# A seam between two stages: the merge's loads are issued in the SSM stage, TensorE goes on without a meeting, and the projections are reordered

## The chip, the cores and the metric

The kernel runs on one NeuronCore of a Trainium2 chip, in one launch. The metric is the device time of an execution in microseconds, the median of several runs. The core has five engines that run their own instruction lists and meet only at semaphores: TensorE (PE, matmuls), VectorE (DVE), ScalarE (ACT), GpSimd (POOL) and SyncE (SP, which here issues every DMA). All data is fp32.

## What is computed

The reference is a first block, a mixer and a mixture of experts, followed by two layers of another block. The change lies in the mixer of the first block, at its merge. Cut to what matters:

```python
def mixer(hc, hl, p, rows, ctx_out):
    pl = jnp.einsum('bld,de->ble', hl, p['w_in'])
    rw_l, ss_l, gt_l = jnp.split(pl, IN_SPLITS, axis=-1)
    ya_c, ya_l = rwkv_branch(rw_c, rw_l, p, ctx_out)      # (1, 512, 1024)
    yb_c, yb_l = ssm_branch(ss_c, ss_l, p, rows, ctx_out)  # (1, 512, 2048)
    return merge(ya_l, yb_l, gt_l, p)

def merge(ya, yb, gates, p):
    ga, gb = jnp.split(jax.nn.sigmoid(gates), 2, axis=-1)
    ya = jnp.einsum('blc,cd->bld', ya, p['proj_a'])
    yb = jnp.einsum('blc,cd->bld', yb, p['proj_b'])
    return jnp.einsum('bld,de->ble', ga * ya + gb * yb, p['w_out'])
```

## The kernel before

The program is a row of stages: start, RWKV, SSM, merge, experts (MoE), and the two layers of the second block. At the end of a stage every engine calls `Port.meet`: it drains, raises its own end count and waits for the end counts of all engines. SyncE waits for all of them at the start of its part of the next stage.

**The stages around the change.** The RWKV stage writes its output to a DRAM buffer, `yad` (8 x 128 x 512). The SSM stage (`ssm_sync`, `ssm_tensor`, `ssm_vector` and so on) follows one list of steps, `ssm_order`, that all engines read. In it four groups of heads are convolved and scanned; a group's result is transposed and stored to `ybd` by `read` steps 4 to 7, a quarter of it each. SyncE does the store. Behind the last group's projection come 16 `mgate` blocks, the merge's gate projections: for each, TensorE does 8 matmuls, ScalarE copies the block out, SyncE stores it to `gmd`. The last of them share the list with the `read` steps of group 3, and the stage ends with a short chain: `yvar` on VectorE, `yrstd` on ScalarE, `dg` on VectorE, four matmuls with `ones` on TensorE (`yrstd`), and VectorE's copy of their result to `k.rb`.

**The merge stage** (`merge_sync`, `merge_tensor`, `merge_vector`, `merge_scalar`). For each of eight row blocks d of the output, TensorE computes `pa` d (8 matmuls of 128x128 by 128x512 over `yaT`) and `pb` d (16 matmuls over `ybT`), each into one of eight PSUM banks. VectorE multiplies both by their sigmoid gates, adds them into `mT[d]` and so frees the two banks. When all eight are there TensorE does the output projection `out` with four weight tiles `wo`. The profile has two records for each of these fp32 matmuls.

**What sets the order.** SyncE issues in program order and stops at each wait. Weights go through a `Ring`, slots of the area `wreg` used in turn: a load into a slot waits until the block that last used it is done. The SSM stage has two slots of 4096 words, the first two thirds of `wreg`; the last third holds its scan buffers. The merge has six slots of 2048 words over the same area. `gates(d)` loads the two gate blocks of d into one of two pairs of buffers and so waits for `mT[d-2]`. In the SSM stage two groups of buffers (`b.groups`) serve the four heads' groups in turn; groups 0 and 2 use the first, groups 1 and 3 the second.

Of the kernel before, what the change touches and what calls it, by code (L numbers as in the profile page):

```python
# [195 lines left out]
class Port:  # L196
# [5 lines left out]
    def wait_ge(self, line, *event):  # L202
# [4 lines left out]
        if self.seen.get(line.name, 0) < count:  # L207
            self.seen[line.name] = count
            self.e.wait_ge(line.sem, count)

    def meet(self, mine, stage):

        self.e.drain().then_inc(self.k.end[mine].up(stage), 1)
        for e in self.k.end:
            self.wait_ge(self.k.end[e], stage)

# [107 lines left out]
class Ring:  # L324


    def __init__(self, sp, areas):
        self.sp, self.areas, self.until, self.i = sp, areas, [None] * len(areas), 0

    def load(self, key, src, *until):  # L330
        i, k = self.i, self.sp.k
        self.i = (i + 1) % len(self.areas)
        if self.until[i]:
            self.sp.wait_ge(*self.until[i])
        self.until[i] = until
        dst = self.areas[i][:, 0:src.shape[1]]
        self.sp.e.dma_start(dst, src).then_inc(k.wline[i].up16(*(key if isinstance(key, tuple) else (key,))), 16)
        k.slot[key] = (dst, k.wline[i])


class Words:
# [45 lines left out]
def v3(ap, n):  # L387
    return ap.rearrange("p (a b) -> p a b", b=n)
# [80 lines left out]
def fetch(sp, dst, src, name):  # L469

    sp.e.dma_start(dst, src).then_inc(sp.k.line(name).up16(name), 16)
# [1004 lines left out]
def ssm_map(k):  # L1476
    b, m, extra, spare = Bag(), k.mem(k.mark1), k.mem(NC1 + NCOL + 8192), k.mem(k.mark0)
    b.hp = v3(m(4096), 512)
    k.rb_at = m.top
    b.dtb, b.na, b.dd = m(64), m(64), m(32)  # L1480
    b.dt, b.dA, b.sc, b.ecum, b.edec, b.etot = (m(384) for _ in range(6))
    b.ss = m(16)
    b.o2 = [m(768) for _ in range(2)]
    b.groups = []
    for _ in range(2):
        o = Bag()
        o.bcm, o.ccm, o.btok = m(768), m(512), m(768)
        o.xt, o.z, o.y = v3(m(3072), 512), v3(m(2048), 512), v3(m(2048), 512)
        b.groups.append(o)
    b.ysum = [m(512) for _ in range(2)]  # L1490
    b.ysq, b.yd = m(512), m(512)
    b.yo = [m(512) for _ in range(2)]
    b.stage = [m(512) for _ in range(2)]
    b.xd, b.xe = ([extra(512) for _ in range(2)] for _ in range(2))
    b.cbm = [extra(128) for _ in range(2)]
    b.h = [extra(512) for _ in range(2)]
    b.dg = extra(512)
    b.LB, b.Wt = ([spare(1024) for _ in range(2)] for _ in range(2))
    b.order = ssm_order()
    k.rb = k.mem(k.rb_at)(512)  # L1500
    return b
# [82 lines left out]
def ssm_sync(k, sp):  # L1584
    b, T, P = k.ss, k.T, k.proj
    for e in k.end:
        sp.wait_ge(k.end[e], "rwkv")
    fetch(sp, b.dtb, k.row("dtb"), "dtb")
    fetch(sp, b.na, k.row("alog"), "alog")
    fetch(sp, b.dd, k.row("ssmd"), "ssmd")  # L1590
    for name, *z in b.order:
        if name == "mgate" and z[1] == 3:
            t, _ = z
            sp.wait_ge(P.act, "mgate", t)
            sp.e.dma_start(k.gmd[t], b.stage[t % 2]).then_inc(k.kept[t % 2].up16("gate", t), 16)
        if name == "dt" or name == "conv" and z[1:] in ([3, 3], [5, 3]) or name == "z" and z[1:] == [3, 1] or (
                name == "mgate" and z[0] % 4 == 3 and z[1] == 3):
            load = next(k.loads, None)
            if load:
                k.ring.load(*load)  # L1600
        elif name == "read" and z[1] > 3:
            g, q = z[0], z[1] - 4
            sp.wait_ge(k.tail.dve, "out", g, q)
            sp.e.dma_start(k.ybd[4 * g + q], b.yo[q % 2]).then_inc(k.stored[q % 2].up16("yb", g, q), 16)


def ssm_tensor(k, pe):
    b, M, P, tail, c = k.ss, k.main, k.proj, k.tail, k.c
    for line in (M.dve, M.act, M.pool):
        pe.wait_ge(line, "hp")  # L1610
    free = {}
    pb, banks = Banks(pe, 0, 4, free), Banks(pe, 4, 8, free)
    at = {}
# [110 lines left out]
    for name, *z in b.order:  # L1724
        if name == "dt":
            ps = banks.take("dt")
            w, loaded = k.slot["wdt"]
            w = v3(w, 64)
            pe.wait_ge(loaded, "wdt")
            for i in range(6):  # L1730
                for kk in range(8):
                    last = pe.mm(ps[:, 64 * i:64 * i + 64], hp_token(k, kk, i), w[:, kk, :], kk == 0, kk == 7)
            last.then_inc(M.pe.up("dt"), 1)
            banks.give("dt", M.dve, "dt")
        elif name == "decay_sum":
            n, = z
            ps = banks.take((name, n))
            pe.wait_ge(M.dve, "dA")
            for i in range(6):
                for d in range(2):  # L1740
                    a = 64 * i + 32 * d
                    last = pe.mm(ps[:, a:a + 32], c[(("up", "lo"), ("los", "ups"), ("ones", "ones"))[n][d]],
                                 b.dA[:, a:a + 32], True, True)
# [13 lines left out]
    ps = banks.take("yrstd")  # L1757
    pe.wait_ge(M.dve, "dg")
    for i in range(4):
        last = pe.mm(ch(ps, i), c["ones"], ch(b.dg, i), True, True)  # L1760
    last.then_inc(M.pe.up("yrstd"), 1)
    pe.meet("pe", "ssm")


def ssm_vector(k, v):
# [100 lines left out]
    for i in range(4):  # L1866
        v.ts(M.dve, ch(b.dg, i), c["ident"], s4[:, i:i + 1], MUL, event=("dg",) if i == 3 else ())
    v.wait_ge(M.pe, "yrstd")
    v.copy(M.dve, k.rb.rearrange("p (r c) -> p c r", c=64), k.pair("yrstd").rearrange("p (c r) -> p c r", r=8))
    v.meet("dve", "ssm")  # L1870


# [131 lines left out]
def merge_map(k):  # L2004
    b, m = Bag(), k.mem(k.rb_at + 512)
    b.g1 = m(1024)
    sa = [m(512)]
    b.x, b.mT, b.yaT, b.ybT = v3(m(4096), 1024), v3(m(4096), 512), v3(m(4096), 512), v3(m(8192), 512)
    sa.append(m(512))
    b.sig = [sa, [m(512) for _ in range(2)]]  # L2010
    b.npo, b.ss, b.scr, b.n2p = m(1024), m(8), m(1024), m(1024)
    back = k.mem(k.mark0)
    k.x, k.h2 = v3(back(4096), 1024), v3(back(4096), 1024)
    k.mark4 = k.mark0 + 4096
    b.n2g, b.n2s = back(1024), back(1024)
    assert back.top <= k.rb_at
    return b


def merge_sync(k, sp):  # L2020
    b, T, M = k.mg, k.T, k.main
    for e in k.end:
        sp.wait_ge(k.end[e], "ssm")
    ring = Ring(sp, [k.wreg[:, 2048 * i:2048 * i + 2048] for i in range(6)])

    def load(name, d):
        ring.load((name, d), T[name][d], M.pe, "branch", d, 1)

    def gates(d):
        if d > 1:  # L2030
            sp.wait_ge(M.dve, "mT", d - 2)
        for br in range(2):
            sp.e.dma_start(b.sig[br][d % 2], k.gmd[2 * d + br]).then_inc(k.line(f"gate_in{d % 2}_{br}").up16("gate", d), 16)

    load("pa", 0)
    for line in k.stored:
        sp.wait_ge(line)
    fetch(sp, b.yaT, k.yad.rearrange("k p t -> p k t"), "yaT")
    for line in k.kept:
        sp.wait_ge(line)  # L2040
    load("pb", 0)
    fetch(sp, b.ybT, k.ybd.rearrange("k p t -> p k t"), "ybT")
    gates(0)
    for name in ("pa", "pb"):
        load(name, 1)
    gates(1)
    fetch(sp, b.x, T["x"].rearrange("(i p) d -> p i d", p=128), "x2")
    sp.wait_ge(k.line("mrow"))
    fetch(sp, b.g1, k.mrow_bc(2048, 1024), "g1")
    fetch(sp, b.npo, k.row("n1post"), "npo")  # L2050
    fetch(sp, b.n2g, k.mrow_bc(4096, 1024), "n2g")
    fetch(sp, b.n2p, k.row("n2pre"), "n2p")
    fetch(sp, b.n2s, k.mrow_bc(3072, 1024), "n2s")
    for d in range(2, 8):
        for name in ("pa", "pb"):
            load(name, d)
        gates(d)
    for n in range(4):
        ring.load(("wo", n), T["wo"][n], M.pe, "out", 3)


def merge_tensor(k, pe):
    b, M = k.mg, k.main
    banks = Banks(pe, 0, 8)
    for d in range(8):
        for br, (name, src, nk, source) in enumerate((("pa", b.yaT, 8, "yaT"), ("pb", b.ybT, 16, "ybT"))):
            w, loaded = k.slot[name, d]
            w = v3(w, 128)
            ps = banks.take(("branch", d, br))
            pe.wait_ge(loaded, name, d)  # L2070
            pe.wait_ge(k.line(source), source)
            for kk in range(nk):
                last = pe.mm(ps, w[:, kk, :], src[:, kk, :], kk == 0, kk == nk - 1)
            last.then_inc(M.pe.up("branch", d, br), 1)
            banks.give(("branch", d, br), M.dve, "branch", d, br)
    for i in range(4):
        ps = banks.take(("out", i), 2)
        pe.wait_ge(M.dve, "mT", 7)
        for n in range(4):
            w, loaded = k.slot["wo", n]  # L2080
            w = v3(w, 256)
            pe.wait_ge(loaded, "wo", n)
            for kk in range(8):
                last = pe.mm(ps[:, 256 * n:256 * n + 256], b.mT[:, kk, 128 * i:128 * i + 128], w[:, kk, :], kk == 0, kk == 7)
        last.then_inc(M.pe.up("out", i), 1)
        banks.give(("out", i), M.dve, "out", i)
    pe.meet("pe", "merge")
# [1400 lines left out]
```

## Time and profile before

| | us |
|---|---|
| median of three runs | 5094.85 |
| lowest and highest of them | 5084.24, 5099.88 |
| the profiled execution, its own time | 5083.77 |
| its span, first to last instruction | 5081.8 |
| TensorE busy | 4611.8 (91%) |
| VectorE, ScalarE, GpSimd busy | 2088.4, 1336.1, 430.9 |

The profile is of one execution. Its times count from the start of the span. TensorE's ends are modelled, so a busy stretch is not a stretch at peak. A wait is named by the engine or the DMA that ended it. The granted clock is given as a share of the full 2.4 GHz. Names such as `lower` and `upper` are the two halves of SBUF, not single tiles.

### The profile page before, as it was taken

What the parts mean: (1) busy time and instruction counts of PE and PEld (TensorE: products, weight loads), DVE (VectorE), ACT (ScalarE), POOL (GpSimd) and SP (SyncE); (2) the same over time, 40 slices, a digit from 0 to 9 for tenths busy, and PEclk for the clock granted to TensorE, in tenths of its full rate; (3) what the DMA queues carried; (4) which work ended last, traced back from release to release, by engine and by line L of the source; (5) the groups of instructions that cost most, each with busy time, mean ns of one, the idle gap of its engine ahead of it and who ended that gap; (6) DMA issues with size and microseconds to landing.
All of it is one profiled execution on the core that took longest, in us unless ns stands there. A gap on an engine that the chain in (4) does not pass through costs nothing.

```text
span 5081.8 us, 85359 instructions
## 1 busy us (share of the span) xinstructions
PE 4611.8 (91%) x36404; PEld 2838.7 (56%) x36404; DVE 2088.4 (41%) x3866; ACT 1336.1 (26%) x2486; POOL 430.9 (8%) x385
## 2 busy tenths in 40 slices
PE   7899889988989898979997999999999999989999
PEld 3566666666555553464443544444777544444777
DVE  3555555553355542130112237453333237453333
ACT  2333333342222211010001124341222124241322
POOL 0121111110223230000000000010000000010000
PEclk9999999998999999989999999999999999999999
DMA  5200000000111124229997211123221211123221
GB/s 227 80 19 19 5 18 19 3 26 13 42 48 44 42 77 174 101 118 376 408 408 312 85 62 46 46 87 133 98 85 35 98 63 46 46 81 140 86 97 50
DMA packets 76818, 503.33 MB, mean 99 GB/s; under 512 B 9480, under 2 KB 10008, under 8 KB 34328
## 3 DMA queue, kind: packets, MB, share of 16 engines
q1 hardware_dynamic: 76440, 497.88, 25.5%
q8 instruction: 287, 4.70, 0.4%
q14 instruction: 91, 0.75, 0.0%
HBM read 472.66 MB, written 25.19 MB: 98 GB/s over the span
## 4 chain that ended last, share of the span: by engine, by line
PE 78%; DVE 8%; issue 6%; DMA 3%; ACT 3%; POOL 1%; SPq 0%; PEldq 0%; PEld 0%; DVEq 0%; ACTq 0%; POOLq 0%
PE ps L224 75%; PE ps L227 3%; DMA upper<-in_ew 2%; DVE upper L243 2%; ACT upper L282 2%; DVE upper L259 1%; DVE upper L235 1%; POOL upper L3394 1%; DVE lower L235 1%; DVE upper L251 1%; ACT lower L282 1%; DVE lower L243 1%; DVE upper L239 0%; DMA upper<-ybd 0%; DVE lower L239 0%
## 5 line engine op out<-in xcount | busy, mean ns | idle before, releaser
L224 PE MATMUL ps<-lower 128*128 128x512 f32 (+12 forms) x7024 | 1935.0, 444 | 66.3 <-issue 22.8
L224 PEld LDWEIGHTS ps<-lower 128*128 128x128 f32 (+3 forms) x7024 | 958.4, 188 | 783.4 <-issue 611.4
L224 PE MATMUL ps<-upper 64*64 64x64 f32 (+7 forms) x15552 | 823.7, 257 | 148.6 <-DVE upper L251 46.0
L282 ACT ACTIVATE upper<-ps 128x512 f32<-128x512 f32 (+5 forms) x967 | 444.5, 491 | 1766.8 <-PE ps L224 1297.6
L224 PEld LDWEIGHTS ps<-upper 64*64 64x64 f32 (+4 forms) x15552 | 591.8, 144 | 451.8 <-issue 220.3
L224 PE MATMUL ps<-lower,upper 64*64 64x64 f32 (+6 forms) x7536 | 723.4, 315 | 51.6 <-DMA lower<-in_ada 20.2
L224 PE MATMUL ps<-rounded 128*128 128x512 f32 x3072 | 718.2, 396 | 30.7 <-DVE rounded L235 23.1
L224 PEld LDWEIGHTS ps<-rounded 128*128 128x128 f32 x3072 | 582.0, 190 | 166.0 <-ACT rounded L282 26.3
L224 PEld LDWEIGHTS ps<-lower,upper 64*64 64x64 f32 (+3 forms) x7536 | 383.4, 144 | 338.4 <-issue 268.3
L282 ACT ACTIVATE upper<-upper 128x256 f32<-128x256 f32 (+12 forms) x695 | 361.9, 529 | 726.9 <-DVE upper L255 186.5
L224 PE MATMUL ps<-upper,lower 128*128 128x512 f32 (+4 forms) x1584 | 481.4, 474 | 24.8 <-DMA upper<-yad 11.7
L224 PEld LDWEIGHTS ps<-upper,lower 128*128 128x128 f32 (+1 forms) x1584 | 248.1, 197 | 247.4 <-issue 229.9
L259 DVE COPY_PREDICATED upper<-lower,ps 128x256 f32<-128x256 uint8 (+2 forms) x576 | 246.4, 457 | 323.9 <-PE ps L224 288.3
L251 DVE COPY upper<-ps 128x64 f32<-128x64 f32 (+9 forms) x423 | 166.8, 405 | 455.9 <-PE ps L224 423.2
L235 DVE TENSOR_TENSOR rounded<-lower,rounded 128x512 fp32r<-128x512 f32 (+2 forms) x136 | 200.8, 1477 | 257.0 <-ACT rounded L282 256.8
L235 DVE TENSOR_TENSOR upper<-upper,ps 128x512 f32<-128x512 f32 (+1 forms) x136 | 108.5, 798 | 452.9 <-PE ps L224 442.0
L282 ACT ACTIVATE rounded<-lower 128x512 fp32r<-128x512 f32 (+2 forms) x136 | 171.7, 1262 | 404.8 <-PE ps L224 270.0
L227 PE MATMUL ps<-lower,upper 128*128 128x128 f32 (+1 forms) x1204 | 188.7, 290 | 84.0 <-ACT upper L282 39.0
L227 PEld LDWEIGHTS ps<-lower,upper 128*128 128x128 f32 (+1 forms) x1204 | 145.2, 147 | 177.1 <-issue 74.5
L282 ACT ACTIVATE lower<-ps 128x512 f32<-128x512 f32 (+1 forms) x174 | 102.2, 592 | 379.9 <-PE ps L224 350.2
L243 DVE SCALAR_TENSOR_TENSOR upper<-ps,lower,upper 128x511 f32<-128x511 f32 (+1 forms) x208 | 130.1, 625 | 134.1 <-ACT upper L282 128.4
L3381 POOL COPY upper<-lower 128x512 f32<-128x512 f32 x8 | 5.0, 631 | 1948.5 <-PE ps L224 1947.7
(81 smaller groups left out, 2139.0 us busy)
## 6 DMA issues: line engine op xcount, KB each, us to landing
lower<-in_ew SPq DMA_DIRECT2D x144, 1024.0 KB, 10.5
upper<-in_ew SPq DMA_DIRECT2D x48, 1024.0 KB, 13.5
lower<-in_b0f SPq DMA_DIRECT2D x16, 2048.0 KB, 7.9
lower<-in_b1f SPq DMA_DIRECT2D x16, 2048.0 KB, 8.0
upper<-in_ada SPq DMA_DIRECT2D x18, 1024.0 KB, 6.2
lower<-in_wrkv SPq DMA_DIRECT2D x8, 1728.0 KB, 7.5
lower<-in_b0g SPq DMA_DIRECT2D x8, 1536.0 KB, 6.6
gad<-upper SPq DMA_DIRECT2D x48, 256.0 KB, 2.0
```

The source lines that it names most:

```text
L224: return self.e.matmul(out, lhsT, rhs, start=start, stop=stop)
L227: return self.e.transpose(out, in_, self.ident[0:n, 0:n])
L235: self.e.tensor_tensor(out, a, b, op).then_inc(line.up(*event), 1)
L243: self.e.scalar_tensor_tensor(out, a, s, b, op0, op1).then_inc(line.up(*event), 1)
L251: self.e.tensor_copy(out, a).then_inc(line.up(*event), 1)
L259: self.e.copy_predicated(out, mask, data).then_inc(line.up(*event), 1)
L282: self.e.activation(out, in_, func, bias=bias, scale=scale, accum_out=accum).then_inc(line.up(*event), 1)
L3381: g.e.tensor_copy(b3[:, :, 0:64], v3(b.kv[:, i, :], 128)[:, :, 0:64]).then_inc(tail.pool.up(), 1)
L3394: g.e.tensor_tensor(y, y, r, SUB).then_inc(o.lane.pool.up("less", *o.u), 1)
```

## The change

1. `Port.meet` is split: `leave` drains and raises the engine's end count, `meet` does this and waits. At the end of the SSM stage TensorE only leaves. Its PSUM banks are carried over (`k.free`), so that the merge waits for a bank where it takes one; VectorE's copy to `k.rb` gets an event, `rb`, for the bank of `yrstd`.
2. `yaT` is loaded in the SSM stage, behind the last `ybd` store of group 2, into the memory of the first group of buffers, which nobody needs from there on. SyncE waits before it for the squares of group 2 and for all its stores to `yad` and `ybd` so far.
3. The merge's weight ring is begun in the SSM stage: `pa` 0 and 1 behind the store of gate block 11, `pa` 2 and `pb` 0 behind that of gate block 15. The slots are those of `wreg` that are free by then, in the order 2, 3, 0, 1, 4, 5, with semaphores of their own.
4. The projections run in another order, three `pa` ahead: `pa` 0, 1, 2, then `pb` 0, `pa` 3, `pb` 1, `pa` 4, up to `pb` 4, `pa` 7, `pb` 5, 6, 7. Their loads follow the same order.

```diff
+    def leave(self, mine, stage):
+        self.e.drain().then_inc(self.k.end[mine].up(stage), 1)
     def meet(self, mine, stage):
-        self.e.drain().then_inc(self.k.end[mine].up(stage), 1)
+        self.leave(mine, stage)
         for e in self.k.end:
             self.wait_ge(self.k.end[e], stage)
...
@@ ssm_sync
-            load = next(k.loads, None)
-            if load:
-                k.ring.load(*load)
+            if name != "mgate" or z[0] < 11:
+                k.ring.load(*next(k.loads))
+            elif z[0] == 11:
+                merge_begin(k, sp)
+                merge_load(k)
+                merge_load(k)
+            else:
+                merge_load(k)
+                merge_load(k)
...
             sp.e.dma_start(k.ybd[4 * g + q], b.yo[q % 2]).then_inc(k.stored[q % 2].up16("yb", g, q), 16)
+            if z == [2, 7]:
+                sp.wait_ge(k.tail.act, "square", 2, 3)
+                for line in k.stored:
+                    sp.wait_ge(line)
+                fetch(sp, k.mg.yaT, k.yad.rearrange("k p t -> p k t"), "yaT")
@@ ssm_tensor
-    pe.meet("pe", "ssm")
+    banks.give("yrstd", M.dve, "rb")
+    k.free = free
+    pe.leave("pe", "ssm")
@@ merge_map
-    b.x, b.mT, b.yaT, b.ybT = v3(m(4096), 1024), v3(m(4096), 512), v3(m(4096), 512), v3(m(8192), 512)
+    b.x = v3(m(4096), 1024)
+    assert k.ss.third[0] <= m.top and m.top + 4096 <= k.ss.third[1]
+    b.yaT, b.mT, b.ybT = v3(m(4096), 512), v3(m(4096), 512), v3(m(8192), 512)
...
+MERGE = [("pa", 0), ("pa", 1), ("pa", 2)] + [t for d in range(8) for t in ([("pb", d), ("pa", d + 3)] if d < 5 else [("pb", d)])]
+
+def merge_begin(k, sp):
+    areas = [k.wreg[:, 2048 * i:2048 * i + 2048] for i in (2, 3, 0, 1, 4, 5)]
+    k.ring = Ring(sp, areas, k.wline[2:8])
+    k.loads = iter([((name, d), k.T[name][d], k.main.pe, "branch", d, int(name == "pb")) for name, d in MERGE] +
+                   [(("wo", n), k.T["wo"][n], k.main.pe, "out", 3) for n in range(4)])
+
+def merge_load(k):
+    k.ring.load(*next(k.loads))
@@ merge_sync
-    load("pa", 0)
-    for line in k.stored:
+    for line in (*k.stored, *k.kept):
         sp.wait_ge(line)
-    fetch(sp, b.yaT, k.yad.rearrange("k p t -> p k t"), "yaT")
-    for line in k.kept:
-        sp.wait_ge(line)
-    load("pb", 0)
     fetch(sp, b.ybT, k.ybd.rearrange("k p t -> p k t"), "ybT")
     gates(0)
-    for name in ("pa", "pb"):
-        load(name, 1)
+    merge_load(k)
+    merge_load(k)
     gates(1)
...
-    for d in range(2, 8):
-        for name in ("pa", "pb"):
-            load(name, d)
-        gates(d)
-    for n in range(4):
-        ring.load(("wo", n), T["wo"][n], M.pe, "out", 3)
+    for t, (name, d) in enumerate(MERGE[6:] + [("wo", n) for n in range(4)]):
+        merge_load(k)
+        if t % 2 and t // 2 + 2 < 8:
+            gates(t // 2 + 2)
@@ merge_tensor
-    banks = Banks(pe, 0, 8)
-    for d in range(8):
-        for br, (name, src, nk, source) in enumerate((("pa", b.yaT, 8, "yaT"), ("pb", b.ybT, 16, "ybT"))):
+    banks = Banks(pe, 0, 8, k.free)
+    for name, d in MERGE:
+        br, src, source = ((0, b.yaT, "yaT"), (1, b.ybT, "ybT"))[name == "pb"]
```

How the instructions stand, first on TensorE at the seam, before. A row is the line, the operation, output and input, the shape, the semaphores it waits for, and a count; `end_*` are the end counts, `weights*` the slots, `yaT` and `ybT` the two fetches, and an engine's name the work of that engine. The first two rows are the last gate block, the next two `yrstd`, the rest the merge:

```order
L224 MATMUL ps<-lower 128x512 [waits proj_act]
L224 MATMUL ps<-lower 128x512 x7
L224 MATMUL ps<-lower 128x128 [waits main_dve,step1_dve]
L224 MATMUL ps<-lower 128x128 x3
L224 MATMUL ps<-upper,lower 128x512 [waits end_pool,weights0,end_act,yaT,end_dve,end_pe]
L224 MATMUL ps<-upper,lower 128x512 x7
L224 MATMUL ps<-upper,lower 128x512 [waits ybT,weights1]
L224 MATMUL ps<-upper,lower 128x512 x15
```

TensorE at the same place in the changed kernel, from `yrstd` on:

```order
L228 MATMUL ps<-lower 128x128 [waits main_dve,step1_dve]
L228 MATMUL ps<-lower 128x128 x3
L228 MATMUL ps<-upper,lower 128x512 [waits yaT,weights2]
L228 MATMUL ps<-upper,lower 128x512 x7
L228 MATMUL ps<-upper,lower 128x512 [waits weights3]
L228 MATMUL ps<-upper,lower 128x512 x7
L228 MATMUL ps<-upper,lower 128x512 [waits weights4,proj_act]
L228 MATMUL ps<-upper,lower 128x512 x7
L228 MATMUL ps<-upper,lower 128x512 [waits ybT,weights5,tail_dve]
L228 MATMUL ps<-upper,lower 128x512 x15
```

The four end counts are gone from the first projection, two more `pa` stand ahead of the first that reads `ybT`, and banks of the SSM stage are waited for one by one.

SyncE from the store of gate block 8 to the first loads behind the meeting, before:

```order
L1595 DMA gmd<-upper 128x512 [waits proj_act] x5
L1604 DMA ybd<-upper 128x512 [waits tail_dve] x2
L1595 DMA gmd<-upper 128x512 [waits proj_act]
L1604 DMA ybd<-upper 128x512 [waits tail_dve] x2
L1595 DMA gmd<-upper 128x512 [waits proj_act] x2
L337 DMA lower<-in_pa 128x1024 [waits end_act,end_pool,end_dve,end_pe]
L471 DMA upper<-yad 128x8x512 [waits stored1,stored0]
L337 DMA lower<-in_pb 128x2048 [waits kept1,kept0]
L471 DMA upper<-ybd 128x16x512
L2033 DMA lower<-gmd 128x512
L2033 DMA upper<-gmd 128x512
```

The same stretch of SyncE in the changed kernel (the fetch of `yad` stands earlier, between the last `ybd` store of group 2 and the third gate store):

```order
L1604 DMA gmd<-upper 128x512 [waits proj_act] x4
L342 DMA lower<-in_pa 128x1024 x2
L1604 DMA gmd<-upper 128x512 [waits proj_act]
L1619 DMA ybd<-upper 128x512 [waits tail_dve] x2
L1604 DMA gmd<-upper 128x512 [waits proj_act]
L1619 DMA ybd<-upper 128x512 [waits tail_dve] x2
L1604 DMA gmd<-upper 128x512 [waits proj_act] x2
L342 DMA lower<-in_pa 128x1024
L342 DMA lower<-in_pb 128x2048
L476 DMA upper<-ybd 128x16x512 [waits stored0,stored1,end_pool,kept0,end_act,kept1,end_dve,end_pe]
L2068 DMA lower<-gmd 128x512
L2068 DMA upper<-gmd 128x512
```

Three `pa` and one `pb` load have moved ahead of the meeting, and `ybd` is the first transfer behind it.

## Rows read from the trace of the kernel before

**Rows 1.** The page: the span, and busy time with its share and instructions.

```profile
span 5081.8 us, 85359 instructions
...
PE 4611.8 (91%) x36404; PEld 2838.7 (56%) x36404; DVE 2088.4 (41%) x3866; ACT 1336.1 (26%) x2486; POOL 430.9 (8%) x385
```

**Rows 2.** TensorE's waits, 1950 to 2200: total, times, longest (us).

```profile
PE ps L224 <- DMA upper<-yad: 11.7, 1, 11.7
PE ps L224 <- DMA upper<-ybd: 4.5, 1, 4.5
```

**Rows 3.** TensorE's timeline, 1960 to 2170: start, duration (us), what, [idle before].

```profile
1965.76 1.93 PE L224 MATMUL ps<-lower 128*128 128x128 f32 x8 [2.75 <-DVE lower L239]
1979.41 8.87 PE L224 MATMUL ps<-upper,lower 128*128 128x512 f32 x16 [11.72 <-DMA upper<-yad]
1992.78 159.87 PE L224 MATMUL ps<-upper,lower 128*128 128x512 f32 x368 [4.50 <-DMA upper<-ybd]
2154.35 15.99 PE L224 MATMUL ps<-lower,upper 128*128 128x256 f32 x73 [1.71 <-DVE upper L235]
```

**Rows 4.** SyncE's DMA issues, 1780 to 2170.

```profile
1827.41 0.32 SPq L1604 DMA_DIRECT2D ybd<-upper  x1
1839.20 10.07 SPq L1595 DMA_DIRECT2D gmd<-upper  x2
...
1968.86 0.33 SPq L337 DMA_DIRECT2D lower<-in_pa  x1
...
1970.35 0.58 SPq L471 DMA_DIRECT2D upper<-ybd  x1
```

**Rows 5.** DMA issues, 1750 to 2130: count, KB each, us to landing.

```profile
upper<-ybd SPq DMA_DIRECT2D x1, 4096.0 KB, 22.3
...
ybd<-upper SPq DMA_DIRECT2D x8, 256.0 KB, 2.0
...
upper<-yad SPq DMA_DIRECT2D x1, 2048.0 KB, 10.0
```

**Rows 6.** Stretches: us, busy us of each engine, granted clock, DMA share, GB/s.

```profile
1829.00:1839.00 10.00, 10.00 (x39) 5.62 (x38) 5.20 (x8) 1.48 (x2) 4.96 (x4) 1.00 0.01 2
...
1968.80:1992.70 23.90, 8.87 (x16) 3.62 (x16) 0.00 (x0) 0.00 (x0) 0.00 (x0) 0.70 0.97 349
1979.40:1992.70 13.30, 8.87 (x16) 3.60 (x16) 0.00 (x0) 0.00 (x0) 0.00 (x0) 0.87 1.03 389
```

**Rows 7.** Stretches around the seam, for the granted clock (third from the end).

```profile
1963.00:1965.70 2.70, 0.01 (x1) 0.00 (x0) 1.15 (x4) 1.24 (x3) 0.00 (x0) 1.00 0.26 97
1965.70:1967.80 2.10, 1.93 (x8) 1.66 (x8) 0.07 (x1) 0.00 (x0) 0.00 (x0) 0.55 0.00 0
...
1979.40:1983.00 3.60, 3.59 (x5) 1.54 (x6) 0.00 (x0) 0.00 (x0) 0.00 (x0) 0.51 1.01 393
...
1992.70:1996.30 3.60, 3.52 (x5) 1.62 (x6) 0.00 (x0) 2.54 (x3) 0.00 (x0) 0.57 1.04 422
```

**Rows 8.** VectorE's timeline, 1964 to 2050.

```profile
1967.73 1.02 DVE L251 COPY lower<-ps 128x512 f32<-128x512 f32 x1 [2.11 <-PE ps L224]
...
2010.82 0.69 DVE L235 TENSOR_TENSOR lower<-lower,ps 128x512 f32<-128x512 f32 x1
...
2029.08 0.69 DVE L235 TENSOR_TENSOR upper<-upper,ps 128x512 f32<-128x512 f32 x1 [12.19 <-PE ps L224]
...
2049.68 0.69 DVE L235 TENSOR_TENSOR upper<-upper,ps 128x512 f32<-128x512 f32 x1 [12.19 <-PE ps L224]
```

**Rows 9.** TensorE's timeline, 1942 to 1951.

```profile
1943.76 0.66 PE L227 MATMUL ps<-lower,upper 128*128 128x128 f32 x4 [1.12 <-ACT upper L282]
1945.59 5.30 PE L224 MATMUL ps<-lower 128*128 128x512 f32 x8 [1.17 <-DVE upper L239]
```

**Rows 10.** Stretches behind the seam, for the granted clock.

```profile
2155.00:2500.00 345.00, 297.81 (x1495) 172.43 (x1494) 71.11 (x100) 33.62 (x66) 0.00 (x0) 0.93 0.70 284
...
4500.00:5081.80 581.80, 547.01 (x2139) 379.57 (x2137) 218.33 (x270) 149.94 (x198) 9.90 (x16) 0.98 0.26 95
```

More of the change, by code:

```diff
@@ L324, with __init__ @@
 class Ring:
-    def __init__(self, sp, areas):
+    def __init__(self, sp, areas, lines=None):
         self.sp, self.areas, self.until, self.i = sp, areas, [None] * len(areas), 0
+        self.lines = lines or sp.k.wline
     def load(self, key, src, *until):
@@ L336, in load @@
         dst = self.areas[i][:, 0:src.shape[1]]
-        self.sp.e.dma_start(dst, src).then_inc(k.wline[i].up16(*(key if isinstance(key, tuple) else (key,))), 16)
-        k.slot[key] = (dst, k.wline[i])
+        self.sp.e.dma_start(dst, src).then_inc(self.lines[i].up16(*(key if isinstance(key, tuple) else (key,))), 16)
+        k.slot[key] = (dst, self.lines[i])
 class Words:
@@ L1484, in ssm_map @@
     b.groups = []
-    for _ in range(2):
+    for z in range(2):
         o = Bag()
+        if z == 0:
+            at = m.top
+        else:
+            b.third = (at, m.top)
         o.bcm, o.ccm, o.btok = m(768), m(512), m(768)
@@ L1597, in ssm_sync @@
                 name == "mgate" and z[0] % 4 == 3 and z[1] == 3):
-            load = next(k.loads, None)
-            if load:
-                k.ring.load(*load)
+            if name != "mgate" or z[0] < 11:
[4 more added lines that the diff above has]
+                merge_load(k)
+            else:
+                merge_load(k)
+                merge_load(k)
         elif name == "read" and z[1] > 3:
@@ L1868, in ssm_vector @@
     v.wait_ge(M.pe, "yrstd")
-    v.copy(M.dve, k.rb.rearrange("p (r c) -> p c r", c=64), k.pair("yrstd").rearrange("p (c r) -> p c r", r=8))
+    v.copy(M.dve, k.rb.rearrange("p (r c) -> p c r", c=64), k.pair("yrstd").rearrange("p (c r) -> p c r", r=8), "rb")
     v.meet("dve", "ssm")
@@ L2023, in merge_sync @@
         sp.wait_ge(k.end[e], "ssm")
-    ring = Ring(sp, [k.wreg[:, 2048 * i:2048 * i + 2048] for i in range(6)])
-    def load(name, d):
-        ring.load((name, d), T[name][d], M.pe, "branch", d, 1)
     def gates(d):
@@ L2053, in merge_sync @@
     fetch(sp, b.n2s, k.mrow_bc(3072, 1024), "n2s")
-    for d in range(2, 8):
-        for name in ("pa", "pb"):
-            load(name, d)
-        gates(d)
-    for n in range(4):
-        ring.load(("wo", n), T["wo"][n], M.pe, "out", 3)
+    for t, (name, d) in enumerate(MERGE[6:] + [("wo", n) for n in range(4)]):
+        merge_load(k)
+        if t % 2 and t // 2 + 2 < 8:
+            gates(t // 2 + 2)
 def merge_tensor(k, pe):
     b, M = k.mg, k.main
-    banks = Banks(pe, 0, 8)
-    for d in range(8):
-        for br, (name, src, nk, source) in enumerate((("pa", b.yaT, 8, "yaT"), ("pb", b.ybT, 16, "ybT"))):
[L2067 to L2075, printed above, removed]
+    banks = Banks(pe, 0, 8, k.free)
+    for name, d in MERGE:
+        br, src, source = ((0, b.yaT, "yaT"), (1, b.ybT, "ybT"))[name == "pb"]
+        w, loaded = k.slot[name, d]
+        w = v3(w, 128)
+        ps = banks.take(("branch", d, br))
+        pe.wait_ge(loaded, name, d)
+        pe.wait_ge(k.line(source), source)
+        nk = 8 * (br + 1)
+        for kk in range(nk):
+            last = pe.mm(ps, w[:, kk, :], src[:, kk, :], kk == 0, kk == nk - 1)
+        last.then_inc(M.pe.up("branch", d, br), 1)
+        banks.give(("branch", d, br), M.dve, "branch", d, br)
     for i in range(4):
```

## The prediction

> **What bounds the kernel now.** I read first the page's busy row [rows 1]: TensorE is busy 91% of the 5081.8 us span, so a change pays only where TensorE stands still and something else holds it. The change touches one place, the seam between the SSM stage and the merge stage, so the second view is TensorE's waits in that stretch [rows 2]: the two long ones are for DMAs, 11.7 us for `yaT` (yad) and 4.5 us for `ybT` (ybd). The third view is the timeline of TensorE there [rows 3]. The last work of the SSM stage (the `yrstd` matmuls) begins at 1965.76 and ends at 1967.69. Then nothing until 1979.41, when `yaT` is in; 16 records (the 8 matmuls of `pa` 0, two records a matmul) to 1988.28; nothing until 1992.78, when `ybT` is in; then 368 records without a gap to 2152.65. The short idle times beside them, 2.75 us before `yrstd` and 1.71 us before the out projection, wait for other engines and stay. So the merge's projections need 384 records, and once fed they never wait.
>
> Why the two waits are there is seen in SyncE's issues [rows 4]: all loads of the merge start at 1968.86, after the meeting, in the order `pa`, `yaT`, `pb`, `ybT`, and they hold 0.5 + 2.1 + 1.0 + 4.2 = 7.9 MB. `ybT` lands 22.3 us after its issue and `yaT` 10.0 us [rows 5], and the DMAs move 349 GB/s over that stretch (1968.8 to 1992.7), 389 GB/s in its later part [rows 6]. The seam is bound by bytes behind a barrier.
>
> The fourth view is the granted clock [rows 7]. It is 1.00 up to 1965.7, 0.55 in the `yrstd` matmuls behind the 2.75 us gap, 0.51 in the first 3.6 us of `pa` 0, 1.00 after that, and 0.57 again in the first 3.6 us of `pb` 0. That is the lower level (1.2 GHz) twice.
>
> **The change part by part.** The unit is one projection block at the full clock. VectorE finishes one row block (`pa` and `pb` of one d) at 2029.08 and the next at 2049.68 [rows 8]: 20.60 us for 48 records, 0.429 us a record, 6.87 us a `pa` and 13.73 us a `pb`. All 384 records cost 164.8 us.
>
> *Removed.* (a) The wait for `yaT`: 11.72 us. (b) The wait for `ybT`: 4.50 us. (c) The slow clock after each: 16 records took 8.87 us where 16 x 0.429 = 6.87, so 2.00 us; 368 records took 159.87 where 368 x 0.429 = 157.94, so 1.93 us. Together 20.15 us, and all of it is on TensorE's path: the out projection starts only after the last `mT`, 1.71 us behind the last record [rows 3].
>
> *Put back.* (d) TensorE's own handoff. It still drains and raises its end count before `pa` 0, but waits for nobody: `pa` 0's own list is `yaT` and its weights, with no bank in it. VectorE's handoff of the same kind (copy ends 1968.75, first issue of SyncE 1968.86) took 0.11 us [rows 4, 8]. What TensorE needs behind its own drain no row shows; the nearest is its wait for a whole eviction by ScalarE, 1.12 us of idle time [rows 9]. I take 0.2, nearer to VectorE's, which is the same instruction; ends 0 and 1.1. (e) The clock. `yrstd` runs at 0.55 before and after the change, for the gap before it stays (ScalarE's copy and the `dg` chain). A restart with 512-wide matmuls cost 2.0, 1.93 and, at 1945.59, 5.30 - 8 x 0.429 = 1.87 us [rows 3, 9]. If the slow stretch begins with `yrstd`, whose 1.93 us count into it, about half of that is left for `pa` 0: 0.9 us. Ends 0.4 and 2.0 (`yrstd` counts for nothing). Put back: 1.1 us, ends 0.4 and 3.1.
>
> *Does `pa` 0 to 2 find its data?* `yaT` is fetched behind the last `ybd` store of group 2, issued at 1827.41; a store lands in 2.0 us and the next issue of SyncE is at 1839.20 [rows 4, 5]. So the wait on the stores costs SyncE 2 us of a free 11.8, what is queued behind it (the gate stores) is not late, and 2.1 MB at 349 GB/s are in by 1838, over 120 us early; that stretch moves 2 GB/s now [rows 6]. The squares it also waits for are from before 1827. `pa` 0 and 1 (1.0 MB, 3 us + 2 to land) go out behind the store of gate block 11, with four gate blocks still to come; a gate block takes TensorE 6.9 us, so they are in before the next store is issued behind them. `pa` 2 and `pb` 0 go out behind the last gate store, at about 1964.5. The store itself stays ahead of them. Cost of all of it: nothing, and if the cover failed it would be a store late by some 3 to 5 us, whose reader waits two blocks later.
>
> *Does `pb` 0 find `ybT`?* This is the step on which the gain hangs. TensorE starts `pa` 0 at 1967.9 and is through three blocks at 1967.9 + 20.6 + 0.9 = 1989.4. `ybT` still waits for all ends (VectorE's is last, 1968.8), so it goes out at about 1968.9 with `pa` 2 and `pb` 0 (1.57 MB) partly ahead of it. Early bound: 4.19 MB at 389 GB/s, 10.8 us, + 2.0 to land: 1981.7. Late bound: all 5.77 MB still to move at 349 GB/s, 16.5 us, + 2.0: 1987.4. Both are before 1989.4, by 2.0 to 7.7 us. I take no wait, and for the range a wait of up to 3.
>
> The Trainium skill speaks to this. DMA: Bandwidth & Descriptors (Where 436 GB/s comes from) gives about 358 GB/s as what one core draws from HBM; [rows 6] show 389 here, so the trace goes above it; by the page `ybT` alone would take 11.7 us, and the sum would be the same. The same page (Queues, rings and completion order) says that transfers of one queue start in order but a later one may finish its write before an earlier one, so that the order of issue promises nothing about arrival. Here each block waits on its own count, and the rule changes only how much of the later traffic slips ahead of `ybT`, which the late bound covers.
>
> *Three row blocks ahead.* From the ninth block on, a bank must be free. Counted from `pa` 0's start, the ninth block (`pa` 5) begins at 75.5 us, 2043; its bank needs `branch` 0 0, which VectorE did at 2010.82 even before [rows 8], held by the late n2 rows, which now have 3.7 MB less ahead of them. The tightest later one is `pb` 6 at 137 us, which needs VectorE's step for block 4, done when `pb` 3 is, at 98. Weights: six slots as before; `pa` 4 and `pb` 2 are asked for behind the setup loads and ahead of the next gate wait, needed at 2024 and later. `wo` 2 and 3 go out behind the gate wait of block 7 (`mT` 5, at 139 us) and are needed at 166; 1.0 MB at 349 GB/s is 3 us + 2. Nothing there reaches TensorE. VectorE, ScalarE and GpSimd keep their rows and waits; after `pb` 7 the tail of 1.71 us is the same.
>
> **Sum.** 20.15 - 0.2 - 0.9 = 19.05 us off. `branch` 7 ends at about 2133.6 in place of 2152.65; the profiled execution's span goes from 5081.8 to 5062.8, its own time from 5083.8 to 5064.7. That execution stands 11.1 us under the median of the three runs (5094.85), which lie 15.6 us apart. The prediction is against the median: 5094.85 - 19.05 = 5075.8. A difference of 0.3% is 15.3 us, about what a measurement of this kernel can tell from no change.
>
> **The rivals.**
> *A, the forecast:* both waits go, 16 to 20 us off. For it: 2 to 8 us of margin on `ybT`, over 100 us on `yaT`.
> *B, `ybT` comes late:* the wait moves to `pb` 0. For it: before, `ybT` needed 22.3 us; the same flight from 1968.9 would land it at 1991.2, a wait of 1.8 us and perhaps a slow restart of 1.9: 15.3 off. If the setup traffic behind it took an equal share of the engines, half the 389 GB/s, 21.6 + 2 us: 1992.5, 3.1 us and 1.9 of clock, 14.0 off: 5081. Against it: the 22.3 us of before held 3.7 MB more ahead of `ybT`.
> *C, the change doesn't do what it says:* something else holds TensorE to 1979 or so, such as a bank of the SSM stage that is freed late, or the drain. A bank of `yrstd` is freed by VectorE's copy at 1968.75; if it were the first one taken, 1.1 us. For more I find no row. Price if `yaT` alone were covered and `ybT` came as before: 13.7 off, 5081.
> *D, slower:* the clock elsewhere. The granted clock is 0.93 in 2155 to 2500 and 0.98 in the last 582 us [rows 10], so each later stage has slow stretches behind its gaps. Everything behind the seam now begins 19 us earlier, and if how many of those gaps end in a slow stretch depends on when they fall, the loss moves with no change in work. The price so far is the spread of unchanged runs, 15.6 us; to end slower it must exceed the 19 us saved, that is over 1.2 times the whole spread, and 34 us for slower by 0.3%. A shift by 20 that costs 25 gives 5101. Against it: the gaps themselves keep their length.
>
> **How the numbers follow.** A 0.80, B 0.12, C 0.05, D 0.03. In A the saving is 16 to 20 us and the two medians carry some 5 us of spread between them, so a good six in seven of A read as faster by over 0.3% (0.69), and the rest as within 0.3%; B and C read as within mostly, 0.02 of them as faster. Faster 0.71, within 0.26, slower 0.03. The range: from 20 us off and 8 of spread, 5066 less a little, to 14 off (B) and 5 of spread, 5086: 5065 to 5087.
>
> **What would show it.** (a) TensorE's timeline: `yrstd` and `pa` 0 with under 1.2 us between them near 1968, and no wait for yad. (b) No wait for ybd before `pb` 0, which starts near 1989; `ybT` lands 13 to 18 us after an issue at 1968.9. (c) Granted clock back at 1.00 within about 2 us of `pa` 0's start, and no second fall. (d) 384 records from near 1967.9 to 2133.6 with no gap for a bank or a weight. (e) The yad fetch issued near 1829.8 and SyncE's next gate store still at 1839. It is wrong if `ybT` lands after 1990, if gate stores or `ybd` stores hold ScalarE or VectorE in the SSM stage, or if the stages behind 2134 take another time than before.

## The result and the profile after

| | before | changed |
|---|---|---|
| median, us | 5094.85 (7 runs, 5084.24 to 5100.0) | 5069.47 (7 runs, 5058.34 to 5080.57) |
| ratio, 95% interval | | 0.9958, 0.9948 to 0.9969 |
| the profiled execution's span, us | 5081.8 | 5069.8 |

The changed kernel is faster by 0.42% (21 us by the ratio, 25 us by the medians). The prediction was 5075.8, between 5065 and 5087.

TensorE's waits in the same stretch as [rows 2], 1950 to 2200, in the changed kernel:

```profile
PE ps L228 <- DVE lower L243: 2.8, 1, 2.8
PE ps L228 <- DVE upper L239: 1.6, 1, 1.6
PE ps L228 <- ACT upper L286: 1.1, 1, 1.1
PE ps L228 <- issue: 0.3, 1, 0.3
```

Both DMA waits are gone, and nothing stands in their place but 0.3 us of issue. TensorE's timeline there, against [rows 3]:

```profile
1957.78 7.13 PE L228 MATMUL ps<-lower 128*128 128x512 f32 x16 [1.12 <-ACT upper L286]
1967.66 1.93 PE L228 MATMUL ps<-lower 128*128 128x128 f32 x8 [2.75 <-DVE lower L243]
1969.85 165.71 PE L228 MATMUL ps<-upper,lower 128*128 128x512 f32 x384 [0.26 <-issue]
2137.11 33.26 PE L228 MATMUL ps<-lower,upper 128*128 128x256 f32 x153 [1.55 <-DVE upper L239]
```

All 384 records run in one piece. To compare kernels I measure the **seam** from the first row here, the start of the last gate block, to the last, the out projection. Before, the gate block began at 1955.87 and the out projection at 2154.35: 198.5 us. Now 2137.11 - 1957.78 = 179.3 us. That is 19.15 us less.

SyncE's issues, against [rows 4], and the landing of the two fetches, against [rows 5] (issues first, then count, KB and us to landing):

```profile
1829.31 0.32 SPq L1619 DMA_DIRECT2D ybd<-upper  x1
1831.40 0.37 SPq L476 DMA_DIRECT2D upper<-yad  x1
1841.11 10.07 SPq L1604 DMA_DIRECT2D gmd<-upper  x2
...
1970.78 0.38 SPq L476 DMA_DIRECT2D upper<-ybd  x1
```

```profile
upper<-ybd SPq DMA_DIRECT2D x1, 4096.0 KB, 14.3
...
upper<-yad SPq DMA_DIRECT2D x1, 2048.0 KB, 9.0
```

The fetch of `yad` waits 2.1 us for the stores and the next gate store comes 11.8 us after the `ybd` store, as before. `ybT` lands at 1985.1; `pb` 0 begins some 21.5 us after `pa` 0, at 1991.3.

The granted clock, against [rows 7] (third from the end):

```profile
1967.80:1970.00 2.20, 1.94 (x9) 1.68 (x10) 0.37 (x1) 0.00 (x0) 0.00 (x0) 0.50 0.92 337
1970.00:1973.00 3.00, 3.00 (x6) 1.42 (x7) 0.65 (x1) 0.00 (x0) 0.00 (x0) 0.80 0.80 298
1985.00:1992.00 7.00, 7.00 (x17) 3.04 (x16) 0.00 (x0) 3.50 (x5) 0.00 (x0) 1.00 1.03 410
```

It is at the lower level in `yrstd` and for about 1.4 us of `pa` 0 (the 0.80 over 3 us is 1.2 us at half the clock), and doesn't fall again before the out projection.

The span fell by only 12.0 us, not 19.15. The rest lies outside the seam: the gate block began 1.9 us later than in the profile of before, and from the out projection to the end it took 5069.8 - 2137.11 = 2932.7 us where it was 2927.4. How far such parts move by themselves, the repeats below show.

### The profile page after: what moved, and what is told of

Its sections match the earlier page's. It is cut to its first block, busy times and chain, and to the rows that moved or that the text cites. A ratio compares the mean times of both kernels' runs of the same rounds, so it can differ in the third digit from the quotient of the medians.

```text
span 5069.8 us, 85359 instructions
## 1 busy us (share of the span) xinstructions
PE 4620.2 (91%) x36404; PEld 2845.7 (56%) x36404; DVE 2088.0 (41%) x3866; ACT 1336.0 (26%) x2486; POOL 431.0 (9%) x385
## 4 chain that ended last, share of the span: by engine, by line
PE 79%; DVE 8%; issue 6%; DMA 3%; ACT 3%; POOL 1%; SPq 0%; PEldq 0%; PEld 0%; DVEq 0%; ACTq 0%; POOLq 0%
PE ps L228 76%; PE ps L231 3%; DMA upper<-in_ew 2%; DVE upper L247 2%; ACT upper L286 2%; DVE upper L263 1%; DVE upper L239 1%; POOL upper L3423 1%; DVE lower L239 1%; DVE upper L255 1%; DVE lower L247 1%; ACT lower L286 1%; DVE upper L243 0%; DVE lower L243 0%; DMA lower<-in_ada 0%
```

## The experiments

All edits are to the changed kernel. Every seam is read as above, from the gate block (7.13 us, 16 records) to the out projection. The kernels `e1` to `e4` and `e6` to `e8` ran once each, at 5066.0 to 5088.8 us; beside a spread of some 20 us between executions those times decide nothing, and only their seams are compared.

**The changed kernel again**, twice, and the kernel before again.

> The changed kernel once more, unedited. The seam is measured from the start of the last pair of gate blocks on TensorE to the first matmul of the out projection: 198.5 us in the kernel before (1955.87 to 2154.35), 179.3 us in the changed one (1957.78 to 2137.11). Theory (the gain is the seam's own 19.1 us, the rest is spread between executions): the seam is 179.3 again within 0.3 us, while the stages in front of it and behind it differ from the first profile by several us either way. Rival (the stages behind the seam really take some 5 us more, since they begin elsewhere in the clock's pattern): from the out projection to the end 2932.7 us again, where the kernel before took 2927.4.

> The kernel before once more, unedited, for its profile. Theory (stages away from the seam differ between executions of one kernel): the seam is 198.5 us again within 0.3 us, and the part behind the out projection's start differs from the first profile's 2927.4 us by some us. Rival (that part is fixed by the program): 2927.4 within 0.5 us.

> The changed kernel unedited, on the same chip and in the same rounds as the version with yrstd inside pa 0. Theory (the gain is the seam's 19.1 us, in whatever state the rest is): ratio to the kernel before 0.9962 within its interval, 19 us. Rival (the stages behind give some of it back): 0.998 or more. Seam 179.3 us.

| | seam | in front of it | behind it | ratio to before (95%) |
|---|---|---|---|---|
| before | 198.5 | 1955.9 | 2927.4 | |
| before_again | 198.6 | 1950.4 | 2930.0 | |
| changed | 179.3 | 1957.8 | 2932.7 | 0.9958 (0.9948 to 0.9969) |
| after_again | 179.3 | 1955.8 | 2932.9 | 0.9974 (0.9962 to 0.9986) |
| after_third | 179.3 | 1964.0 | 2929.3 | 0.9970 (0.9959 to 0.9981) |

The seam repeats within 0.1 us. What is in front of it moves by 8.2 us between executions of one kernel, and what is behind by 2.6 and 3.6 us. The three ratios are 21, 13 and 15 us, 16.6 on the mean; each interval holds 19.15, the second only at its edge. The ratio of `after_third` (0.9970) lies between its two expectations, 0.9962 and 0.998, and decides little. Whether the part behind is really some microseconds longer is open: unedited, 2927.4 and 2930.0 before against 2932.7, 2932.9 and 2929.3. The eight edited kernels, nine runs, gave 2926.5 to 2934.3, with the shortest and the longest both among versions of the changed kernel. That is no ground for a cost of the change, nor does it exclude one of 2 or 3 us.

**The old order.**

```diff
-MERGE = [("pa", 0), ("pa", 1), ("pa", 2)] + [...]
+MERGE = [(name, d) for d in range(8) for name in ("pa", "pb")]
```

> The changed kernel with the projections in the old order (pa 0, pb 0, pa 1, pb 1, ...), loads too; all else as changed. Theory (three blocks ahead is what covers ybT): pa 0 ends at about 7.8 us after it starts, ybT lands 14.3 us after its issue, so TensorE waits 7.5 us at pb 0 and pays a second slow restart of 1.9 us: seam 179.3 + 9.4 = 188.7 us. Rival (the early loads and the missing meeting carry the gain, the order is worth little, since ybT has less ahead of it anyway): under 182 us.

TensorE's timeline of this kernel:

```profile
1964.92 7.13 PE L228 MATMUL ps<-lower 128*128 128x512 f32 x16 [1.12 <-ACT upper L286]
1974.80 1.95 PE L228 MATMUL ps<-lower 128*128 128x128 f32 x8 [2.75 <-DVE lower L243]
1977.01 7.76 PE L228 MATMUL ps<-upper,lower 128*128 128x512 f32 x16 [0.26 <-issue]
1993.66 160.73 PE L228 MATMUL ps<-upper,lower 128*128 128x512 f32 x368 [8.89 <-DMA upper<-ybd]
2156.10 14.27 PE L228 MATMUL ps<-lower,upper 128*128 128x256 f32 x65 [1.71 <-DVE upper L239]
```

Seam 191.2 us, 11.9 more than the changed kernel (9.4 expected). `ybT` took 15.6 us in place of 14.3, so the wait is 8.9 us, and the restart cost 160.73 - 157.94 = 2.8 us, the dearest seen. With the order taken back the rest of the change still gains 7.3 us. That 11.9 of 19.15 us go with the order doesn't make it the main part: `e3` below loses as much without the early `yaT`.

**The meeting kept.**

```diff
-    pe.leave("pe", "ssm")
+    pe.meet("pe", "ssm")
```

> The changed kernel with TensorE's meeting at the end of the SSM stage kept; early loads and new order as changed. Theory (the meeting itself costs only what VectorE's copy takes beyond yrstd): TensorE starts pa 0 about 1.0 us later, behind VectorE's end, with at most 1 us more of slow clock: seam 180.3 to 181.3 us. Rival (the meeting is the main cost and the loads would be hidden without its removal): over 185 us.

```profile
1951.58 7.13 PE L228 MATMUL ps<-lower 128*128 128x512 f32 x16 [1.12 <-ACT upper L286]
1961.47 1.92 PE L228 MATMUL ps<-lower 128*128 128x128 f32 x8 [2.75 <-DVE lower L243]
1964.59 166.94 PE L228 MATMUL ps<-upper,lower 128*128 128x512 f32 x384 [1.20 <-DVEq L213]
2133.09 37.15 PE L228 MATMUL ps<-lower,upper 128*128 128x256 f32 x171 [1.55 <-DVE upper L239]
```

The granted clock at the start of `pa` 0 in this kernel (third from the end):

```profile
1964.60:1968.00 3.40, 3.40 (x4) 1.47 (x5) 0.00 (x0) 0.00 (x0) 0.00 (x0) 0.50 0.78 249
```

Seam 181.5 us, just above the 180.3 to 181.3 expected. The wait before `pa` 0 is now for VectorE's end count (`DVEq`). The meeting is worth 2.2 us: 1.20 of wait in place of 0.26, and 1.2 us more of slow clock (166.94 against 165.71). The rival is out.

**`yaT` late**: the fetch out of `ssm_sync`, put ahead of that of `ybT` in `merge_sync`.

> The changed kernel with yaT fetched behind the meeting, first of SyncE's loads there and just ahead of ybT, as late as before; all else as changed. Theory: yaT lands 8 to 10 us after its issue, so TensorE stands some 10 us before pa 0 and restarts slowly (2.0 against 0.9 us); ybT lands some 5 us later than now, but pb 0 begins 10 us later, so no second wait: seam 179.3 + 10 + 1.1 = 190.4 us, between 188.5 and 191. Rival (with three pa loaded and no meeting, the fetch of yaT is mostly covered or ybT now waits as well): under 185, or over 195 us.

```profile
1949.93 7.13 PE L228 MATMUL ps<-lower 128*128 128x512 f32 x16 [1.12 <-ACT upper L286]
1959.82 1.91 PE L228 MATMUL ps<-lower 128*128 128x128 f32 x8 [2.75 <-DVE lower L243]
1972.79 167.15 PE L228 MATMUL ps<-upper,lower 128*128 128x512 f32 x384 [11.05 <-DMA upper<-yad]
2141.48 28.73 PE L228 MATMUL ps<-lower,upper 128*128 128x256 f32 x132 [1.55 <-DVE upper L239]
```

Seam 2141.48 - 1949.93 = 191.5 us, half a microsecond above the range that I gave. TensorE waits 11.05 us once and never for `ybT`. The late `yaT` costs 12.2 us.

**Two `pa` ahead** in place of three.

```diff
+MERGE = [("pa", 0), ("pa", 1)] + [t for d in range(8) for t in ([("pb", d), ("pa", d + 2)] if d < 6 else [("pb", d)])]
```

> The changed kernel with two pa ahead of the first pb in place of three. Theory (ybT lands 14.3 us after its issue, 15.3 us after pa 0 starts; two pa last 13.7 + 0.9 = 14.6 us): TensorE waits about 0.6 us once and the clock stays: seam 179.9 us, between 179.3 and 180.5. Rival (the third block is needed in full): a wait of 3 us or more and a slow restart, over 183 us.

```profile
1973.76 14.62 PE L228 MATMUL ps<-upper,lower 128*128 128x512 f32 x32 [0.26 <-issue]
1989.67 151.30 PE L228 MATMUL ps<-upper,lower 128*128 128x512 f32 x352 [1.28 <-DMA upper<-ybd]
2142.52 27.65 PE L228 MATMUL ps<-lower,upper 128*128 128x256 f32 x127 [1.55 <-DVE upper L239]
```

The granted clock behind the wait for `ybT` (third from the end):

```profile
1989.70:1993.00 3.30, 3.30 (x8) 1.56 (x9) 0.00 (x0) 2.53 (x3) 0.00 (x0) 1.00 1.00 405
```

The gate block was at 1961.67: seam 180.8 us, 1.5 more (0.6 expected; `ybT` took 14.8 us, not 14.3). The clock stayed up behind the 1.28 us. So the third block buys 1.5 us, and with it some 6 us of margin are left.

**Setup loads first**: `x`, `g1` and the four others ahead of `ybT` in `merge_sync`.

> The changed kernel with the six setup loads of the merge (x, g1, npo, n2g, n2p, n2s, 4.7 MB) issued ahead of ybT in place of behind it. Theory (ybT's flight is set by the bytes ahead of it): ybT lands 12 us later, at about 1997 on the changed kernel's clock, so TensorE waits 5.8 us at pb 0 and restarts slowly for 1.9: seam 187.0 us. Rival (transfers of one queue don't hold each other up, arrival doesn't follow issue): ybT's landing moves by less than 5 us and the seam stays at 179.3.

SyncE's issues and TensorE's timeline of this kernel:

```profile
1974.09 0.38 SPq L476 DMA_DIRECT2D upper<-in_x  x1
...
1977.43 0.48 SPq L476 DMA_DIRECT2D upper<-ybd  x1
```

```profile
1961.07 7.13 PE L228 MATMUL ps<-lower 128*128 128x512 f32 x16 [1.12 <-ACT upper L286]
...
1973.16 21.49 PE L228 MATMUL ps<-upper,lower 128*128 128x512 f32 x48 [0.26 <-issue]
2001.59 146.23 PE L228 MATMUL ps<-upper,lower 128*128 128x512 f32 x336 [6.93 <-DMA upper<-ybd]
2149.38 20.96 PE L228 MATMUL ps<-lower,upper 128*128 128x256 f32 x96 [1.55 <-DVE upper L239]
```

Seam 188.3 us (187.0 expected). `ybT` landed 24.0 us after its issue, which was 3.3 us later for the issues ahead of it: 30.5 us after `yrstd` began, against 17.4 in the changed kernel. 13.1 us for 4.7 MB is 360 GB/s, where 349 to 389 GB/s [rows 6] make 12.1 to 13.5 us. So `ybT` arrived as late as the bytes ahead of it make it, and the rival is out. The Trainium skill, DMA: Bandwidth & Descriptors (Queues, rings and completion order), promises no order of arrival. In this trace the large transfers landed in the order of their issue: `x` 9.1 us after 1974.09 and `ybT` 24.0 us after 1977.43.

**Each part alone.** Late loads, meeting kept; in `e7` only `yaT` is early, in `e8` only the order is new.

> One part alone: yaT fetched in the SSM stage as in the changed kernel; the meeting, the late weight loads and the old order as in the kernel before. Theory (the two waits stand in a row behind the same bytes, so removing the first alone mostly lengthens the second): pa 0's weights are in 3.3 us after the meeting, pa 0 runs, and pb 0 then waits for ybT, which lands some 5 us earlier than before since 2.1 MB less is ahead of it: seam about 193.4 us in place of 198.5, a gain of 5 us. Rival (the parts add: the wait for yaT and its slow clock go, 13.7 us): 184.8 us.

> The other part alone: the new order of the projections, with all loads behind the meeting (pa 0, yaT, pa 1, pa 2, pb 0, ybT) and the meeting kept. Theory: the wait of 11.7 us for yaT stays, and three pa cover ybT, which has 1.0 MB more ahead of it and still lands before pb 0: the 4.5 us and 1.9 us of clock go: seam 192.0 us, a gain of 6.5. Together with the early yaT alone that is 11.5, so the two parts give some 7 us more together than one by one. Rival (the longer queue ahead of ybT eats the cover): over 195 us.

The early `yaT` alone:

```profile
1952.40 7.13 PE L228 MATMUL ps<-lower 128*128 128x512 f32 x16 [1.12 <-ACT upper L286]
1962.29 1.92 PE L228 MATMUL ps<-lower 128*128 128x128 f32 x8 [2.75 <-DVE lower L243]
1968.92 8.96 PE L228 MATMUL ps<-upper,lower 128*128 128x512 f32 x16 [4.71 <-DMA lower<-in_pa]
1982.93 159.85 PE L228 MATMUL ps<-upper,lower 128*128 128x512 f32 x368 [5.04 <-DMA upper<-ybd]
2144.49 25.71 PE L228 MATMUL ps<-lower,upper 128*128 128x256 f32 x118 [1.71 <-DVE upper L239]
```

The order alone:

```profile
1956.69 7.13 PE L228 MATMUL ps<-lower 128*128 128x512 f32 x16 [1.12 <-ACT upper L286]
...
1979.91 166.96 PE L228 MATMUL ps<-upper,lower 128*128 128x512 f32 x384 [11.41 <-DMA upper<-yad]
2148.42 21.82 PE L228 MATMUL ps<-lower,upper 128*128 128x256 f32 x100 [1.55 <-DVE upper L239]
```

Seams 192.1 and 191.7: gains of 6.4 us (5 expected) and 6.8 us (6.5 expected). With the first wait gone alone, a wait of 4.71 us for `pa` 0's weights takes its place, the slow restart stays, and the second wait is slightly longer than before (5.04 us against 4.50). One by one the two parts give 13.1 us; the whole change gives 19.15. The 6.0 us between them also hold the early weights and the missing meeting (2.2 us, `e2`). No run takes the early weights alone away, so their share is not measured by itself.

**What was left: `yrstd` inside `pa` 0.** The 2.75 us before `yrstd` and the slow clock behind it.

```diff
@@ ssm_tensor: the yrstd matmuls become k.yrstd(), called later
     pe.leave("pe", "ssm")
@@ merge_tensor
             last = pe.mm(ps, w[:, kk, :], src[:, kk, :], kk == 0, kk == nk - 1)
+            if (name, d, kk) == ("pa", 0, 3):
+                k.yrstd()
```

> The changed kernel with the yrstd matmuls moved from the end of the SSM stage into pa 0, behind its fourth matmul; TensorE leaves the stage right behind the last gate block. The result is the same. Theory (the 2.75 us wait before yrstd and the slow clock it brings are what is left at the seam): the wait goes (2.75), yrstd takes about 1.0 us in place of 1.93, and pa 0 runs at the full clock (0.9): seam 179.3 - 4.6 = 174.7 us. ybT goes out at about the same time as now and pb 0 begins 4.6 us earlier, at 21.6 us after pa 0's start, so the margin of 5.3 us on ybT shrinks to about 1 us, but holds. Rival (ybT is then late, or the interruption in pa 0 costs as much as the gap): 178 us or more.

> The version with the yrstd matmuls inside pa 0 once more, in the same rounds as the changed kernel. Theory: seam 174.9 us, 4.4 us under the changed kernel's; ratio to the kernel before 0.9954, that is 23.6 us. Since 4.4 us is 0.09%, less than an interval of a few rounds, the times may not part the two, the seam does. Rival (no gain beyond the changed kernel): seam 179 us.

The first run's timeline of TensorE, and the granted clock over `yrstd` (third from the end):

```profile
1954.62 7.13 PE L228 MATMUL ps<-lower 128*128 128x512 f32 x16 [1.12 <-ACT upper L286]
1962.02 3.67 PE L228 MATMUL ps<-upper,lower 128*128 128x512 f32 x8 [0.26 <-issue]
1965.52 1.05 PE L228 MATMUL ps<-lower 128*128 128x128 f32 x8
1966.41 161.53 PE L228 MATMUL ps<-upper,lower 128*128 128x512 f32 x376
2129.50 40.81 PE L228 MATMUL ps<-lower,upper 128*128 128x256 f32 x188 [1.55 <-DVE upper L239]
```

```profile
1965.50:1966.50 1.00, 1.00 (x10) 0.97 (x9) 0.00 (x0) 0.00 (x0) 0.00 (x0) 1.00 0.95 311
```

Seam 174.9 us in both runs (the second 1962.38 to 2137.26), 4.4 less than the changed kernel, with no wait for `ybT`. `yrstd` takes 1.05 us at the full clock, where it took 1.93. By times it beats both kernels: 0.9950 (0.9935 to 0.9964) and 0.9941 (0.9925 to 0.9956) against the kernel before, and in the second comparison its median is 5063.7 beside 5074.9 for the changed kernel. Of those 11 us the seam explains 4.4; the rest is outside it, where executions differ by as much.

## Why the prediction was right

- **The removed waits.** 11.72, 4.50, 2.00 and 1.93 us, 20.15 in all: gone. The sum was made on the right stretch, and the seam fell by 19.15 us where it said 19.05: 20.15 less the handoff of 0.26 and the clock of 0.9, and 0.16 more off the tail.
- **The handoff (d)** was taken as 0.2 and measured 0.26, a drain and a restart of TensorE without a meeting. The meeting kept gives 1.20.
- **The clock (e)** was taken as 0.9 and measured 165.71 - 164.8 = 0.9. That fits its reading, that the slow stretch begins with `yrstd` and `yrstd` counts into it. But this holds only for the short handoff, which the prediction didn't say: in `e2`, with 1.20 us between the two in place of 0.26, `pa` 0 paid 166.94 - 164.8 = 2.1 us, as much as after a long wait, so there `yrstd` saved it nothing. `e5` confirms the cause from the other side: without the 2.75 us gap the clock stays at 1.00.
- **`ybT` in time.** On the changed kernel's own clock, 1.9 us later than before, the bounds are 1983.6 and 1989.3, the need 1991.3, the landing 1985.1. The margin was 6.2 us, and `e4`, `e1` and `e6` show it used up: by 1.3 us with one block less, 8.9 with two less, 6.9 with 4.7 MB more ahead.
- **Banks, weights, gates, stores.** No wait for any of them in 384 records. VectorE began its products at 2003.42 in place of 2010.82 [rows 8]. The tail behind `pb` 7 was taken as 1.71 and is 1.55.
- **Rivals B and C** did not happen. `e6` shows what a late `ybT` costs, brought on by bytes ahead of it. B's own reason, that the traffic behind `ybT` takes an equal share, did not show: some 6 MB were issued behind it before it landed, and it took 14.3 us, not 23.6. C's price for `yaT` alone, 13.7 us off, was wrong: `e7` gives 6.4. C left out the wait for `pa` 0's own weights (4.71 us) and half a microsecond more of waiting for `ybT`, and it took the slow restart of 2.0 us as gone, which stayed (8.96 us for 16 records).
- **The rest of the time.** The first median is 6.3 us under the forecast, and the profiled span 7.0 us over its own (5069.8 against 5062.8). The seam is as forecast within 0.1 us, so the 7.0 us lie outside it; the first median can't be divided so, having no trace of its own. That this first comparison came out clear of 0.3% has some luck in it: it gave 0.42%, the two repeats 0.26% and 0.30%. I took 15.6 us for the spread of unchanged runs; over all comparisons the kernel before ran between 5076.9 and 5100.0, 23 us. One of the prediction's own signs of being wrong did appear in the first profile: the stages behind the seam took another time than before, 2932.7 us in place of 2927.4. Unchanged kernels differ there by 2.6 and 3.6 us by themselves, so whether the change adds anything, as rival D feared, stays open; no run separates it.

## What to carry to other kernels

At a barrier, count the bytes that start behind it and the work that needs none of them; put that work first, and start every load whose data and memory are ready before the barrier. The parts belong together: a load made early while the next one stays late mostly moves the wait, so cost the whole row of waits, not each by itself. Where a change is worth less than the spread of the runs, measure the stretch that it touches in the trace: here it repeats within 0.1 us, while whole executions differ by 20.

## What the runs showed that I had not expected

The spread of whole executions begins long before the seam. In the first 200 us, where all kernels here run the same program, the granted clock was 0.90 in the profile of before and 0.80 in that of the changed kernel:

```profile
0.00:200.00 200.00, 151.04 (x1576) 86.73 (x1576) 80.25 (x163) 53.91 (x73) 8.15 (x16) 0.90 0.49 186
```

```profile
0.00:200.00 200.00, 151.62 (x1394) 85.69 (x1396) 76.57 (x153) 51.87 (x69) 8.15 (x16) 0.80 0.49 185
```

The first load for the SSM stage (`wdt`) went out at 1043.9 us in the one and at 1052.7 in the other. Most of the profiles with 0.90 or 0.91 there have it between 1042.5 and 1045.3 (one, `e5_again`, at 1050.8), those with 0.80 to 0.86 between 1046.5 and 1053.3. Part of that was given back by the seam, where the two profiles stood only 1.9 us apart. Why the clock is granted later in some executions no run here shows.

A restart of TensorE with 512-wide matmuls, over 0.429 us a record, cost 1.9 to 2.4 us behind waits of 4.5 to 11.7 us (seven of them, in the kernel before, `e3`, `e6`, `e7` and `e8`; the last is 166.96 - 164.8 = 2.2), and 2.8 us once (`e1`, behind 8.9 us), so its price doesn't follow the length of the wait. Behind the 1.28 us of `e4` it cost 151.30 - 151.07 = 0.2 us (352 records at 20.60 / 48 us), but behind the 1.17 us at 1945.59 in the kernel before [rows 9] it cost 1.87. Ahead of the wait in `e4` TensorE had been busy without a break for 14.62 us; ahead of the one at 1945.59 it had done 0.66 us of work behind another 1.12 us of idle time. So a short wait alone doesn't tell the price either; what TensorE did before it differs between the two.

An issue by SyncE can itself be held. The first gate load behind `ybT`, 256 KB, took 12.64 us to issue in the kernel before, behind the 7.9 MB of the merge's first loads, and 3.67 us in the changed kernel, where most issues of that stretch take 0.3 to 2 us (first row before, second changed):

```profile
1970.98 12.64 SPq L2033 DMA_DIRECT2D lower<-gmd  x1
1971.20 3.67 SPq L2068 DMA_DIRECT2D lower<-gmd  x1
```

TensorE didn't wait for any load behind these two, so it cost nothing here. What ends such a hold no run here shows.
